# The spatial mixing of a gated block in three products of rounded halves instead of one f32 product

## The chip, the cores and the metric

The kernel runs on one core of a Trainium2 chip. The metric is the device time of one execution in microseconds; of three runs of the kernel before, the median was 1364.89 us (1363.35 to 1366.57).

## What is computed

Two transformer blocks on 512 tokens of width 1024. The change sits in the first layer of the first block, a gated MLP with spatial mixing:

```
u, v, z = split(h @ w_in, 3)                       # each 512 x 2048
u = gelu(u)
v = rms_norm(gelu(v), sgu_g)
v = v.reshape(1, 4, 128, 8, 256)                   # chunks of 128 tokens, 8 groups of 256 columns
mixed = einsum('gts,bcsge->bctge', tril(w_s), v) + b_s
y = u * mixed * silu(z)
return x + gate * (y @ w_out)
```

The mixing multiplies each group's columns of v, chunk by chunk of 128 tokens, with a lower triangular 128x128 matrix.

## The kernel before, in words

The program is written out per engine, with semaphores between the engines; no scheduler moves anything. TensorE, VectorE, ScalarE, GpSimd (called pool in the code) and the DMA queue of SyncE each have their own list of instructions, and each runs its list in order.

Large products are made of rounded halves. A tile a is split into a_hi, its value rounded to the float32r type, and a_lo = a - a_hi, and a product becomes three: hi with hi, hi with lo, lo with hi (`columns`, line 2187, and `split`, line 2178). ScalarE rounds a chunk of weights of 128x2048 (`to_hi`, line 678), VectorE subtracts (`to_lo`, line 1228).

The first layer goes in stages. The v stage makes 8 chunks of v in `v_pair` (line 2296); ScalarE applies gelu and sums the squares (`v_chunk`, line 750). Behind its last chunk ScalarE does four small operations on the statistics (lines 784 to 790), between which VectorE does its own (lines 1462 to 1469). Then comes the uz stage, 16 blocks j (the loop `uz_pair`, two blocks for each u, par = 0 and 1). In each block:

- TensorE (line 2338) waits for the chunk of weights and for free accumulators, makes u and z of 128 columns in two banks, 24 products of 512 columns each, then waits for v_staged and does the mixing into turn0 or turn1: for four chunks c of tokens one f32 product with v_stage as stationary and ws_t as moving operand.
- GpSimd (`stage`, line 621) makes the staged tile: v times its reciprocal rms, 128x512, into v_stage0 or v_stage1 by turns. It waits for the mixing of block j - 2 by the code.
- ScalarE (line 793) rounds the next chunk of weights, applies gelu to u into one of two gelu_u, tanh to z, and rounds the result y into y_hi.
- VectorE (line 1472) subtracts for the next chunk of weights (w_lo), does two units of the modulation (ada_units), multiplies the gates (tanh_z, then gelu_u), reads the mixing out of the bank with gain and bias (mixed), multiplies (line 1490), and subtracts y_hi (line 1492).

The triangular mask is put on ws_t by VectorE early in the v stage (line 1449), which raises ws_ready to 1. Ahead of the uz stage stands `pe.wait_ge(ws_ready, 1)` (line 2355). TensorE's `stay_busy` (line 2278) issues products on zeros at the start of the program.

```
for half in range(2):
    columns(G[2 * par + half][:, :], par, half, KT, h_hi, h_lo_of).then_inc(mm_done, 1)
pe.wait_ge(v_staged, j + 1)
ge(pe, mix_freed, j - 1)
for c in range(TB):
    mixed_c = mm((T0, T1)[par][:, P * c:P * c + P], v_stage[par][:, c, :], ws_t[:, u - W_UZ // 2, :], True, True)
mixed_c.then_inc(mix_done, 1)
```

Of the kernel before, what the change touches and what calls it, by code (L numbers as in the profile page):

```python
# [26 lines left out]
P = 128  # L27
TOK = 512
# [126 lines left out]
def program(nc, d):  # L155
# [4 lines left out]
    def at(name, shape, off, dt=F32):  # L160
        return nc.alloc_sbuf_tensor_at(name, shape, dt, offset=off)
# [85 lines left out]
    b_sp = at("b_sp", [P, GROUPS, P], off_blocks)  # L247
    gelu_u = [at(f"gelu_u{s}", [P, TOK], T[2 + s]) for s in range(2)]
    tanh_z = at("tanh_z", [P, TOK], T[4])
    mixed = [at(f"mixed{s}", [P, TOK], T[5 + s]) for s in range(2)]  # L250
    v_stage = [at(f"v_stage{s}", [P, TB, P], T[7 + s]) for s in range(2)]
    v_sq = at("v_sq", [P, TB, 256], T[2])
# [89 lines left out]
    def sem(name):  # L342
        return nc.alloc_semaphore(name)
# [11 lines left out]
    up_done, up_out, gsa_done = sem("up_done"), sem("up_out"), sem("gsa_done")  # L355
    xn_done, one_ready, idle_ready = sem("xn_done"), sem("one_ready"), sem("idle_ready")
    hi_done, lo_done, lo_half_done = sem("hi_done"), sem("lo_done"), sem("lo_half_done")
# [3 lines left out]
    sq_ready, sq_added, qsq_ready = sem("sq_ready"), sem("sq_added"), sem("qsq_ready")  # L361
    qlo_ready, half_zeroed, half_ready = sem("qlo_ready"), sem("half_zeroed"), sem("half_ready")
    sum_done, ln_done, y0_done, half_done = sem("sum_done"), sem("ln_done"), sem("y0_done"), sem("half_done")
# [6 lines left out]
    v_sums_done, v_stat_dve, v_stat_act = sem("v_sums_done"), sem("v_stat_dve"), sem("v_stat_act")  # L370
    v_staged, mix_done, mix_freed = sem("v_staged"), sem("mix_done"), sem("mix_freed")
    gelu_done, tanh_done, uz_done = sem("gelu_done"), sem("tanh_done"), sem("uz_done")
# [76 lines left out]
    def next_chunk(u, par):  # L449
        return (u, 1) if par == 0 else (u + 1, 0)  # L450
# [21 lines left out]
    with block:  # L472
# [146 lines left out]
        @block.gpsimd  # L619
        def _(pool):  # L620
            def stage(j, par):

                ge(pool, mix_done, j - 1)
                nc.gpsimd.tensor_tensor(v_stage[par][:, :, :], v[:, :, bass.ds(j * P, P)],
                                        v_stat[:, 5, :].unsqueeze(2).broadcast_to([P, TB, P]), ALU.mult).then_inc(v_staged, 1)

            def sum_squares(k, total, tile):

                for m in range(1, KT - 1):
                    pool.wait_ge(sq_ready, 8 * k + m + 1)  # L630
                    if m > 1:
                        pool.wait_ge(sq_added, 6 * k + m - 1)
                    nc.gpsimd.tensor_tensor(total, tile(0) if m == 1 else total, tile(m), ALU.add).then_inc(sq_added, 1)

            nc.gpsimd.memset(one_row[:, :], 1.0).then_inc(one_ready, 1)
            nc.gpsimd.memset(idle[:, :].bitcast(F32), 0.0).then_inc(idle_ready, 1)
            nc.gpsimd.memset(half_r[:, :].bitcast(F32), 0.0).then_inc(half_zeroed, 1)
            nc.gpsimd.memset(eps_tile[:, :], EPS)
            nc.gpsimd.memset(ones_r[:, :].bitcast(F32), 1.0).then_inc(ones_ready, 1)
            pool.wait_ge(half_zeroed, 1)  # L640
            pool.wait_ge(ones_ready, 1)
            for e in range(2):
                if e:
                    pool.wait_ge(half_ready, 1)
                part = slice(64 * e, 64 * e + 64)
                nc.gpsimd.memset(half_r[part, part].bitcast(F32), 1.0).then_inc(half_ready, 1)
            pool.wait_ge(half_ready, 2)
            pool.wait_ge(v_stat_dve, 3)
            stage(0, 0)
            stage(1, 1)  # L650
            with pool.Fori(1, AT // 2) as i:
                for par in range(2):
                    stage(2 * i + par, par)

            sum_squares(1, sq_sum[:, :], lambda m: sq_a[m % 2][:, :])

            def quarters(m):

                pool.wait_ge(exp_done, 4 * m + 4)
                ge(pool, spread_done, m)  # L660
                stats = row_stat[:, 0, :, :].rearrange("p k n -> p (k n)").unsqueeze(1).broadcast_to([P, 4, 16])
                nc.gpsimd.tensor_tensor(row_apart[:, :, :], stats, own_quarter.unsqueeze(2).broadcast_to([P, 4, 16]), ALU.mult).then_inc(apart_done, 1)

            pool.wait_ge(blocks_loaded, 16)
            for m in range(QH):
                quarters(m)
            pool.wait_ge(pv_done, 4 * QH)
            nc.gpsimd.memset(wf_hi[:, :, :].bitcast(F32), 0.0).then_inc(wf_zeroed, 1)
            nc.gpsimd.memset(wf_lo[:, :, :].bitcast(F32), 0.0).then_inc(wf_zeroed, 1)
            sum_squares(2, sq_sum[:, :], lambda m: sq[m % 2][:, :])  # L670
            sum_squares(3, sq_sum[:, :], lambda m: sq[m % 2][:, :])
# [3 lines left out]
        def _(act):  # L675
# [113 lines left out]
            act.wait_ge(lam_part, 2)  # L789
            nc.scalar.activation(lam_two[:, :], lam_two[:, :], ACT.Exp).then_inc(lam_exp, 1)  # L790


            def uz_pair(u):
                j = 2 * u - W_UZ
                for par in range(2):
                    to_hi(*next_chunk(u, par))
                    act.wait_ge(mm_done, 4 * u + 2 * par + 1)
                    ge(act, uz_done, j + par - 1)
                    nc.scalar.activation(gelu_u[par][:, :], G[2 * par][:, :], ACT.Gelu_apprx_tanh).then_inc(gelu_done, 1)
                    act.wait_ge(mm_done, 4 * u + 2 * par + 2)  # L800
                    ge(act, uz_done, j + par)
                    nc.scalar.activation(tanh_z[:, :], G[2 * par + 1][:, :], ACT.Tanh, scale=0.5).then_inc(tanh_done, 1)
                    act.wait_ge(y_done, j + par + 1)
                    nc.scalar.activation(y_hi[:, j + par, :], mixed[par][:, :], ACT.Copy).then_inc(yhi_done, 1)

# [415 lines left out]
        def _(dve):  # L1221
# [246 lines left out]
            dve.wait_ge(lam_exp, 1)  # L1468
            stt(neg_lam[:, :], lam_two[:, 1:2], -LAM_INIT, lam_two[:, 0:1], ALU.add, ALU.subtract).then_inc(lam_ready, 1)


            def uz_pair(u, cond):
                jj = 2 * u - W_UZ
                g = u - W_UZ // 2
                for par in range(2):
# [6 lines left out]
                    dve.wait_ge(acc_freed, 2 * j + 2)  # L1482
                    stt(gelu_u[par][:, :], tanh_z[:, :], 0.5, gelu_u[par][:, :], ALU.mult, ALU.mult).then_inc(uz_done, 1)
                    dve.wait_ge(mix_done, j + 1)
                    mix = mixed[par][:, :].rearrange("p (c t) -> p c t", c=TB)
                    stt(mix, (T0, T1)[par][:, :].rearrange("p (c t) -> p c t", c=TB), vecs[:, bass.ds(j + G_SGU, 1)],
                        b_sp[:, bass.ds(g, 1), :].broadcast_to([P, TB, P]), ALU.mult, ALU.add).then_inc(mix_freed, 1)
                    dve.wait_ge(mix_freed, j + 1)
                    dve.wait_ge(uz_done, j + 1)
                    nc.vector.tensor_tensor(mixed[par][:, :], mixed[par][:, :], gelu_u[par][:, :], ALU.mult).then_inc(y_done, 1)  # L1490
                    dve.wait_ge(yhi_done, j + 1)
# [682 lines left out]
        def _(pe):  # L2174
# [106 lines left out]

            pe.wait_ge(one_ready, 1)
            pe.wait_ge(c_loaded, 16)
            for n in range(2):
                mm(G[n][:, :], one_row[:, :], c_in[:, TOK * n:TOK * n + TOK], True, True).then_inc(c_spread_in, 1)
            pe.wait_ge(idle_ready, 1)
            stay_busy(6)
# [50 lines left out]
            def uz_pair(u):  # L2338
                jj = 2 * u - W_UZ
                for par in range(2):  # L2340
                    j = jj + par
                    chunk_ready(u, par)
                    if isinstance(u, int):
                        pe.wait_ge(v_gelu_done, 2 * (W_UZ - 2 + par) + 2)
                    else:
                        pe.wait_ge(acc_freed, 2 * j - 2)
                    for half in range(2):
                        columns(G[2 * par + half][:, :], par, half, KT, h_hi, h_lo_of).then_inc(mm_done, 1)
                    pe.wait_ge(v_staged, j + 1)
                    ge(pe, mix_freed, j - 1)  # L2350
                    for c in range(TB):
                        mixed_c = mm((T0, T1)[par][:, P * c:P * c + P], v_stage[par][:, c, :], ws_t[:, u - W_UZ // 2, :], True, True)
                    mixed_c.then_inc(mix_done, 1)

            pe.wait_ge(ws_ready, 1)
            uz_pair(W_UZ // 2)
# [255 lines left out]
            pe.wait_ge(wflo_done, 1)  # L2612
            pe.wait_ge(half_ready, 2)
            pe.wait_ge(acc_freed, 2 * W_Q2 - 16)
# [374 lines left out]
```

## Time and profile before

| what | value |
|---|---|
| median of the runs | 1364.89 us (1363.35 to 1366.57) |
| the profiled execution, by the same measure | 1366.15 us |
| its span, first to last instruction | 1364.4 us |
| matmuls and weight loads | 7883 each |
| DVE, ACT, POOL instructions | 1793, 1261, 55 |
| granted TensorE clock over the span | 1.000 |
| HBM traffic over the span | 132 GB/s |

PE is TensorE's matmul, PEld its weight loads, which overlap the matmuls; DVE is VectorE, ACT ScalarE, POOL GpSimd, SP the queue of SyncE. The duration of a matmul is modelled to its end in the pipeline and overlaps the next one's, so the distance between starts is what one costs in a row of them. An f32 product appears as two records, each with its weight load, a product of rounded values as one. Idle time of an engine that nobody waits for costs nothing. The times of timeline rows are counted from the start of the span.

### The profile page before, as it was taken

How to read it: one execution, taken by the hardware profiler on the slowest of the kernel's cores; microseconds unless marked ns; L12 is line 12 of the kernel's file. 1: busy time of each engine (PE TensorE's matmuls, PEld its weight loads, DVE VectorE, ACT ScalarE, POOL GpSimd, SP SyncE). 2: the span in 40 equal slices, each digit the busy share in tenths (PEclk: the TensorE clock that was granted, in tenths of full speed). 3: DMA queues.
4: the chain of work that ended last, by engine and by line, in shares of the span. 5: the costliest groups of instructions: out<-in, count | busy, mean ns of one | idle time of the engine just before them, and what ended most of it. 6: DMA issues, size and time to landing. Idle time of an engine off the chain costs nothing.

```text
span 1364.4 us, 21359 instructions
## 1 busy us (share of the span) xinstructions
PE 1356.1 (99%) x7883; PEld 1164.0 (85%) x7883; DVE 1060.6 (78%) x1793; ACT 718.5 (53%) x1261; POOL 50.9 (4%) x55
## 2 busy tenths in 40 slices
PE   8999999999999999999999999999999999999999
PEld 6998888888879878888888787887788998998997
DVE  6976677777799788888888867878878965983873
ACT  5744333223357666666664467667646642662561
POOL 0000000000100000000001100000030000000000
PEclk9999999999999999999999999999999999999999
DMA  9995455556753221111221231111131232333232
GB/s 378 388 354 187 178 184 184 184 185 262 292 193 105 79 81 62 63 63 61 65 88 64 93 124 62 62 63 63 37 118 62 94 132 78 103 122 124 77 111 92
DMA packets 35350, 181.51 MB, mean 133 GB/s; under 512 B 4153, under 2 KB 4921, under 8 KB 20930
## 3 DMA queue, kind: packets, MB, share of 16 engines
q1 hardware_dynamic: 34050, 177.95, 35.9%
q10 hardware_dynamic: 1216, 2.44, 0.5%
q8 instruction: 52, 0.85, 0.3%
q14 instruction: 32, 0.26, 0.1%
HBM read 177.74 MB, written 2.11 MB: 132 GB/s over the span
## 4 chain that ended last, share of the span: by engine, by line
PE 89%; DVE 4%; DMA 4%; issue 2%; ACT 1%; SPq 0%; DVEq 0%; ACTq 0%
PE acc L2176 66%; PE turn L2808 7%; PE ada L2176 4%; DMA ada_out<-in_ada 3%; PE turn L2176 3%; PE norm L2176 3%; PE ada L2808 2%; PE acc L2808 2%; PE norm L2808 2%; DVE w_lo L1234 1%; PE turn L2653 1%; PE turn L2499 1%; DVE hk_lo L1226 0%; DVE ada_out L1226 0%; DVE hx L1226 0%
## 5 line engine op out<-in xcount | busy, mean ns | idle before, releaser
L2176 PE MATMUL acc<-h_hi,w_hi 128*128 128x512 f32 x696 | 277.1, 398 | 0.0
L2176 PE MATMUL acc<-h_hi,w_lo 128*128 128x512 f32 x696 | 271.9, 391 | 0.0
L2176 PE MATMUL acc<-h_lo,w_hi 128*128 128x512 f32 x696 | 271.3, 390 | 0.0
L1234 DVE TENSOR_TENSOR w_lo<-w_raw,w_hi 128x2048 fp32r<-128x2048 f32 x58 | 136.4, 2352 | 29.9 <-ACT w_hi L683 29.9
L2176 PEld LDWEIGHTS acc<-h_hi,w_lo 128*128 128x128 f32 x696 | 130.6, 188 | 28.3
L2176 PEld LDWEIGHTS acc<-h_hi,w_hi 128*128 128x128 f32 x696 | 130.8, 188 | 27.0 <-issue 0.4
L2176 PEld LDWEIGHTS acc<-h_lo,w_hi 128*128 128x128 f32 x696 | 130.9, 188 | 25.5
L683 ACT ACTIVATE w_hi<-w_raw 128x2048 fp32r<-128x2048 f32 x60 | 114.4, 1907 | 29.0 <-PE acc L2176 28.2
L2176 PE MATMUL acc<-wv_hi,h_hi 128*128 128x256 f32 x320 | 90.5, 284 | 0.0
L1226 DVE SCALAR_TENSOR_TENSOR x<-acc,mods,x 128x512 f32<-128x512 f32 x48 | 38.7, 814 | 66.6 <-PE acc L2176 66.5
L2176 PE MATMUL acc<-wv_lo,h_hi 128*128 128x256 f32 x320 | 89.2, 280 | 0.0
L2176 PE MATMUL acc<-wv_hi,h_lo 128*128 128x256 f32 x320 | 88.4, 280 | 0.0
L689 ACT ACTIVATE y<-norm,eps_tile 128x512 f32<-128x512 f32 x54 | 37.2, 689 | 63.7 <-PE norm L2176 63.7
L2176 PE MATMUL acc<-gu_lo,w_hi 128*128 128x512 f32 x176 | 68.5, 389 | 0.0
L2176 PE MATMUL acc<-gu_hi,w_hi 128*128 128x512 f32 x176 | 68.5, 389 | 0.0
L2176 PE MATMUL acc<-gu_hi,w_lo 128*128 128x512 f32 x176 | 68.5, 389 | 0.0
L2176 PEld LDWEIGHTS acc<-wv_lo,h_hi 128*128 128x128 f32 x320 | 61.0, 190 | 0.2
L2176 PEld LDWEIGHTS acc<-wv_hi,h_hi 128*128 128x128 f32 x320 | 60.2, 188 | 0.2
L2176 PEld LDWEIGHTS acc<-wv_hi,h_lo 128*128 128x128 f32 x320 | 59.6, 188 | 0.0
L1226 DVE SCALAR_TENSOR_TENSOR ada_out<-ada_out,csil 128x1024 f32<-128x1024 f32 x32 | 38.4, 1221 | 18.3 <-DMA ada_out<-in_ada 18.0
L2176 PE MATMUL acc<-y_hi,w_hi 128*128 128x512 f32 x128 | 50.2, 392 | 0.0
L2176 PE MATMUL acc<-y_hi,w_lo 128*128 128x512 f32 x128 | 49.9, 390 | 0.0
(385 smaller groups left out, 3470.9 us busy)
## 6 DMA issues: line engine op xcount, KB each, us to landing
w_raw<-in_weights SPq DMA_DIRECT2D x102, 1024.0 KB, 4.9
ada_v<-in_ada SPq DMA_DIRECT2D x32, 512.0 KB, 6.1
ada_raw<-in_ada SPq DMA_DIRECT2D x32, 512.0 KB, 5.7
ada_out<-in_ada SPq DMA_DIRECT2D x32, 512.0 KB, 6.4
ada_up<-in_ada_first SPq DMA_DIRECT2D x8, 1024.0 KB, 16.9
w_raw<-in_weights SPq DMA_DIRECT2D x4, 768.0 KB, 4.4
x<-in_x SPq DMA_DIRECT2D x2, 1024.0 KB, 6.1
w_first<-in_weights SPq DMA_DIRECT2D x4, 512.0 KB, 13.6
```

The lines of the kernel that those rows point to most:

```text
L683: nc.scalar.activation(weights_at(u, par)[0][:, 0:used], w_raw[par][:, 0:used], ACT.Copy).then_inc(hi_done, 1)
L689: nc.scalar.activation(y0[:, :], total, ACT.Ln, scale=1.0 / count, bias=eps_col).then_inc(ln_done, 1)
L1226: return nc.vector.scalar_tensor_tensor(out, in0, scalar, in1, op0, op1, **more)
L1234: nc.vector.tensor_tensor(lo[:, 0:used], w_raw[par][:, 0:used], f32(hi[:, 0:used]), ALU.subtract).then_inc(lo_done, 1)
L2176: return nc.tensor.matmul(out, lhsT, rhs, start=start, stop=stop)
L2499: turned = nc.tensor.transpose((T0, T1)[c % 2][:, P * b:P * b + P], s_b[tile][:, lo:lo + P], ident)
L2653: turned = nc.tensor.transpose(T0[:, P * b:P * b + P], s_2[n % 3][:, 0, P * b:P * b + P], ident)
L2808: last = nc.tensor.matmul(out, w_part[:, n, :], a_part[:, n, :], start=start and n + m == 0, stop=stop and n + m == 5, skip_group_check=no ...
```

## The change

The mixing is made of rounded halves like the large products. ws_t gets a rounded half ws_hi (ScalarE) and a remainder ws_lo (VectorE), each raising ws_ready by one. The staged tile gets a rounded half v_stage_hi (ScalarE, semaphore v_rounded) and a remainder v_stage_lo (GpSimd, written over v_stage). TensorE does three products of 128 columns where it did one in f32. The staged tile lies where ws_t was, so the first staging waits for ws_ready = 3, and so does TensorE ahead of the uz stage. v_stage, gelu_u and mixed have one buffer each instead of two. Two semaphores are merged into others (fill_ready, half_ready), with no other effect on the order.

```diff
-    gelu_u = [at(f"gelu_u{s}", [P, TOK], T[2 + s]) for s in range(2)]
-    tanh_z = at("tanh_z", [P, TOK], T[4])
-    mixed = [at(f"mixed{s}", [P, TOK], T[5 + s]) for s in range(2)]
-    v_stage = [at(f"v_stage{s}", [P, TB, P], T[7 + s]) for s in range(2)]
+    gelu_u = at("gelu_u", [P, TOK], T[2])
+    tanh_z = at("tanh_z", [P, TOK], T[3])
+    mixed = at("mixed", [P, TOK], T[4])
+    v_stage = at("v_stage", [P, TB, P], big + 64 * KB)
+    v_stage_lo = at("v_stage_lo", [P, TB, P], big + 64 * KB, F32R)
+    v_stage_hi = at("v_stage_hi", [P, TB, P], big + 66 * KB, F32R)
+    ws_hi = at("ws_hi", [P, GROUPS, P], T[7], F32R)
+    ws_lo = at("ws_lo", [P, GROUPS, P], T[5], F32R)
...
             def stage(j, par):
-                ge(pool, mix_done, j - 1)
-                nc.gpsimd.tensor_tensor(v_stage[par][:, :, :], v[:, :, bass.ds(j * P, P)],
+                ge(pool, mix_done, j)
+                nc.gpsimd.tensor_tensor(v_stage[:, :, :], v[:, :, bass.ds(j * P, P)],
                                         v_stat[:, 5, :].unsqueeze(2).broadcast_to([P, TB, P]), ALU.mult).then_inc(v_staged, 1)
+                pool.wait_ge(v_rounded, j + 1)
+                nc.gpsimd.tensor_tensor(v_stage_lo[:, :, :], v_stage[:, :, :], v_stage_hi[:, :, :].bitcast(F32), ALU.subtract).then_inc(v_staged, 1)
...
             pool.wait_ge(v_stat_dve, 3)
+            pool.wait_ge(ws_ready, 3)
             stage(0, 0)
...
             nc.scalar.activation(lam_two[:, :], lam_two[:, :], ACT.Exp).then_inc(lam_exp, 1)
+            act.wait_ge(ws_ready, 1)
+            nc.scalar.activation(ws_hi[:, :, :], ws_t[:, :, :], ACT.Copy).then_inc(ws_ready, 1)
...
                 for par in range(2):
+                    act.wait_ge(v_staged, 2 * (j + par) + 1)
+                    nc.scalar.activation(v_stage_hi[:, :, :], v_stage[:, :, :], ACT.Copy).then_inc(v_rounded, 1)
                     to_hi(*next_chunk(u, par))
                     act.wait_ge(mm_done, 4 * u + 2 * par + 1)
-                    ge(act, uz_done, j + par - 1)
-                    nc.scalar.activation(gelu_u[par][:, :], G[2 * par][:, :], ACT.Gelu_apprx_tanh).then_inc(gelu_done, 1)
+                    nc.scalar.activation(gelu_u[:, :], G[2 * par][:, :], ACT.Gelu_apprx_tanh).then_inc(gelu_done, 1)
...
             stt(neg_lam[:, :], lam_two[:, 1:2], -LAM_INIT, lam_two[:, 0:1], ALU.add, ALU.subtract).then_inc(lam_ready, 1)
+            dve.wait_ge(ws_ready, 2)
+            nc.vector.tensor_tensor(ws_lo[:, :, :], ws_t[:, :, :], f32(ws_hi[:, :, :]), ALU.subtract).then_inc(ws_ready, 1)
...
-                    pe.wait_ge(v_staged, j + 1)
+                    pe.wait_ge(v_staged, 2 * j + 2)
                     ge(pe, mix_freed, j - 1)
+                    coarse, fine = ws_hi[:, u - W_UZ // 2, :], ws_lo[:, u - W_UZ // 2, :]
                     for c in range(TB):
-                        mixed_c = mm((T0, T1)[par][:, P * c:P * c + P], v_stage[par][:, c, :], ws_t[:, u - W_UZ // 2, :], True, True)
+                        out = (T0, T1)[par][:, P * c:P * c + P]
+                        mm(out, v_stage_hi[:, c, :], coarse, True, False)
+                        mm(out, v_stage_hi[:, c, :], fine, False, False)
+                        mixed_c = mm(out, v_stage_lo[:, c, :], coarse, False, True)
                     mixed_c.then_inc(mix_done, 1)
 
-            pe.wait_ge(ws_ready, 1)
+            pe.wait_ge(ws_ready, 3)
             uz_pair(W_UZ // 2)
```

In the built program the places are these. ScalarE between the v stage and the uz stage; a row is a line of code, the operation, what is written and what is read, and the semaphores it waits for. Before:

```order
L788 ACTIVATE v_stat<-v_stat 128x4 [waits v_stat_act]
L790 ACTIVATE lam_two<-lam_two 128x2 [waits lam_part]
L683 ACTIVATE w_hi_60<-w_raw_53 128x2048 [waits mm_done,w_loaded1]
L799 ACT_TABLE_LOAD
L799 ACTIVATE gelu_u_137<-acc 128x512 [waits mm_done]
L802 ACTIVATE tanh_z<-acc 128x512 [waits mm_done]
```

and with the change:

```order
L796 ACTIVATE v_stat<-v_stat 128x4 [waits v_stat_act]
L798 ACTIVATE lam_two<-lam_two 128x2 [waits lam_part]
L800 ACTIVATE ws_hi<-ws_t 128x1024 [waits ws_ready]
L807 ACTIVATE v_stage_hi<-v_stage 128x512 [waits v_staged]
L691 ACTIVATE w_hi_60<-w_raw_53 128x2048 [waits mm_done,w_loaded1]
L810 ACT_TABLE_LOAD
L810 ACTIVATE gelu_u<-acc 128x512 [waits mm_done]
```

Two roundings stand ahead of that of the next chunk of weights, w_hi.

TensorE at the start of the uz stage (acc are the banks of u and z, turn those of the mixing), with the change; before, the first row waits for the same three semaphores and in place of the twelve turn rows stand four of turn<-ws_t,v_stage:

```order
L2189 MATMUL acc<-h_hi,w_hi_59 128x512 [waits v_gelu_done,lo_done,ws_ready]
L2189 MATMUL acc<-h_lo,w_hi_59 128x512
L2189 MATMUL acc<-h_hi,w_lo_61 128x512
...
L2189 MATMUL turn<-ws_hi,v_stage_hi 128x128 [waits v_staged]
L2189 MATMUL turn<-ws_lo,v_stage_hi 128x128
L2189 MATMUL turn<-ws_hi,v_stage_lo 128x128
```

The wait for ws_ready stands on the first product of the stage in both programs; its value is now 3 where it was 1.

## Rows read from the trace of the kernel before

**Rows 1.** The page: busy us, share of the span and count of instructions, by engine.

```profile
PE 1356.1 (99%) x7883; PEld 1164.0 (85%) x7883; DVE 1060.6 (78%) x1793; ACT 718.5 (53%) x1261; POOL 50.9 (4%) x55
```

**Rows 2.** Stretches: length; busy us of PE, PEld, DVE, ACT, POOL; clock; DMA.

```profile
114.30:304.60 190.30, 190.30 (x904) 159.46 (x903) 133.19 (x162) 60.83 (x74) 16.62 (x16) 1.00 0.48 175
304.60:1364.40 1059.80, 1055.51 (x6245) 904.34 (x6243) 837.54 (x1480) 596.26 (x1066) 32.81 (x28) 1.00 0.28 101
```

**Rows 3.** Timeline of one block, TensorE: start, us, engine, line, operation, out<-in, count.

```profile
196.28 1.06 PE L2176 MATMUL turn<-ws_t,v_stage 128*128 x8
197.09 0.47 PE L2176 MATMUL acc<-h_hi,w_hi 128*128 128x512 f32 x1
...
197.40 0.39 PE L2176 MATMUL acc<-h_lo,w_hi 128*128 128x512 f32 x1
...
197.63 0.40 PE L2176 MATMUL acc<-h_hi,w_lo 128*128 128x512 f32 x1
...
208.92 0.47 PE L2176 MATMUL acc<-h_hi,w_hi 128*128 128x512 f32 x1
```

**Rows 4.** Timeline, TensorE around a product of 96 columns.

```profile
49.28 0.21 PE L2176 MATMUL acc<-ones_r 128*128 128x96 f32 x1
...
49.33 0.35 PE L2176 MATMUL acc<-wv_hi,h_hi 128*128 128x256 f32 x1
...
49.52 0.28 PE L2176 MATMUL acc<-wv_lo,h_hi 128*128 128x256 f32 x1
...
49.63 0.28 PE L2176 MATMUL acc<-wv_hi,h_lo 128*128 128x256 f32 x1
```

**Rows 5.** Timeline, TensorE's weight loads behind two products of 2 columns.

```profile
766.80 0.19 PEld L2176 LDWEIGHTS acc<-xg_hi,w_hi 128*128 128x128 f32 x1
766.91 0.19 PEld L2176 LDWEIGHTS acc<-xg_lo,w_hi 128*128 128x128 f32 x1
```

**Rows 6.** Timelines and one tile: start of the uz stage; operations of 128x1024.

```profile
114.41 0.40 PE L2176 MATMUL acc<-h_hi,w_hi 128*128 128x512 f32 x1
...
118.14 0.19 ACT L790 ACTIVATE lam_two<-lam_two 128x2 f32<-128x2 f32 x1
...
766.26 1.06 ACT L955 ACTIVATE w_hi<-w_raw 128x1024 fp32r<-128x1024 f32 x1 [0.76 <-PE acc L2176]
...
L1449 DVE TENSOR_TENSOR ws_t<-ws_t,consts x1: 1222/1222/1222, 59.6 to 59.6; 128x1024 f32<-128x1024 f32 x1
```

**Rows 7.** The start of the program: timeline of TensorE and its weight loads.

```profile
6.21 2.93 PE L2176 MATMUL ada<-idle 128*128 128x512 f32 x6
8.94 4.64 PE L2176 MATMUL norm<-sq_first,ones_r 128*128 128x512 f32 x8
...
9.81 0.34 PEld L2176 LDWEIGHTS norm<-sq_first,ones_r 128*128 128x128 f32 x1 [0.52 <-DVE sq_first L1421]
10.66 0.34 PEld L2176 LDWEIGHTS norm<-sq_first,ones_r 128*128 128x128 f32 x1 [0.52 <-issue]
11.27 0.19 PEld L2176 LDWEIGHTS norm<-sq_first,ones_r 128*128 128x128 f32 x1 [0.28 <-issue]
...
13.02 4.23 PE L2176 MATMUL ada<-idle 128*128 128x512 f32 x16
18.75 0.45 PE L2176 MATMUL acc<-w_first,h_full 128*128 128x256 f32 x1 [1.50 <-issue]
```

**Rows 8.** Timeline of the same block, the other engines; the last row is of block 15.

```profile
197.52 1.04 POOL L624 TENSOR_TENSOR v_stage<-v,v_stat 128x512 f32<-128x512 f32 x1 [10.79 <-PE turn L2176]
...
198.01 1.11 DVE L1226 SCALAR_TENSOR_TENSOR gelu_u<-tanh_z,gelu_u 128x512 f32<-128x512 f32 x1
...
200.63 0.63 ACT L804 ACTIVATE y_hi<-mixed 128x512 f32 x1 [3.48 <-DVE mixed L1490]
...
209.03 0.69 DVE L1226 SCALAR_TENSOR_TENSOR tanh_z<-tanh_z,acc 128x512 f32<-128x512 f32 x1 [1.26 <-ACT tanh_z L802]
...
304.37 0.69 DVE L1226 SCALAR_TENSOR_TENSOR gelu_u<-tanh_z,gelu_u 128x512 f32<-128x512 f32 x1
```

More of the change, by code:

```diff
@@ L355, in program @@
     up_done, up_out, gsa_done = sem("up_done"), sem("up_out"), sem("gsa_done")
-    xn_done, one_ready, idle_ready = sem("xn_done"), sem("one_ready"), sem("idle_ready")
+    xn_done, fill_ready = sem("xn_done"), sem("fill_ready")
     hi_done, lo_done, lo_half_done = sem("hi_done"), sem("lo_done"), sem("lo_half_done")
@@ L361, in program @@
     sq_ready, sq_added, qsq_ready = sem("sq_ready"), sem("sq_added"), sem("qsq_ready")
-    qlo_ready, half_zeroed, half_ready = sem("qlo_ready"), sem("half_zeroed"), sem("half_ready")
+    qlo_ready, half_ready = sem("qlo_ready"), sem("half_ready")
     sum_done, ln_done, y0_done, half_done = sem("sum_done"), sem("ln_done"), sem("y0_done"), sem("half_done")
@@ L370, in program @@
     v_sums_done, v_stat_dve, v_stat_act = sem("v_sums_done"), sem("v_stat_dve"), sem("v_stat_act")
-    v_staged, mix_done, mix_freed = sem("v_staged"), sem("mix_done"), sem("mix_freed")
+    v_staged, v_rounded = sem("v_staged"), sem("v_rounded")
+    mix_done, mix_freed = sem("mix_done"), sem("mix_freed")
     gelu_done, tanh_done, uz_done = sem("gelu_done"), sem("tanh_done"), sem("uz_done")
@@ L633, in sum_squares @@
                     nc.gpsimd.tensor_tensor(total, tile(0) if m == 1 else total, tile(m), ALU.add).then_inc(sq_added, 1)
-            nc.gpsimd.memset(one_row[:, :], 1.0).then_inc(one_ready, 1)
-            nc.gpsimd.memset(idle[:, :].bitcast(F32), 0.0).then_inc(idle_ready, 1)
-            nc.gpsimd.memset(half_r[:, :].bitcast(F32), 0.0).then_inc(half_zeroed, 1)
+            nc.gpsimd.memset(one_row[:, :], 1.0).then_inc(fill_ready, 1)
+            nc.gpsimd.memset(idle[:, :].bitcast(F32), 0.0).then_inc(fill_ready, 1)
+            nc.gpsimd.memset(half_r[:, :].bitcast(F32), 0.0).then_inc(half_ready, 1)
             nc.gpsimd.memset(eps_tile[:, :], EPS)
             nc.gpsimd.memset(ones_r[:, :].bitcast(F32), 1.0).then_inc(ones_ready, 1)
-            pool.wait_ge(half_zeroed, 1)
+            pool.wait_ge(half_ready, 1)
             pool.wait_ge(ones_ready, 1)
@@ L643, in _ @@
                 if e:
-                    pool.wait_ge(half_ready, 1)
+                    pool.wait_ge(half_ready, 2)
                 part = slice(64 * e, 64 * e + 64)
                 nc.gpsimd.memset(half_r[part, part].bitcast(F32), 1.0).then_inc(half_ready, 1)
-            pool.wait_ge(half_ready, 2)
+            pool.wait_ge(half_ready, 3)
             pool.wait_ge(v_stat_dve, 3)
+            pool.wait_ge(ws_ready, 3)
             stage(0, 0)
@@ L803, in uz_pair @@
                     act.wait_ge(y_done, j + par + 1)
-                    nc.scalar.activation(y_hi[:, j + par, :], mixed[par][:, :], ACT.Copy).then_inc(yhi_done, 1)
+                    nc.scalar.activation(y_hi[:, j + par, :], mixed[:, :], ACT.Copy).then_inc(yhi_done, 1)
             uz_pair(W_UZ // 2)
@@ L1482, in uz_pair @@
                     dve.wait_ge(acc_freed, 2 * j + 2)
-                    stt(gelu_u[par][:, :], tanh_z[:, :], 0.5, gelu_u[par][:, :], ALU.mult, ALU.mult).then_inc(uz_done, 1)
+                    stt(gelu_u[:, :], tanh_z[:, :], 0.5, gelu_u[:, :], ALU.mult, ALU.mult).then_inc(uz_done, 1)
                     dve.wait_ge(mix_done, j + 1)
-                    mix = mixed[par][:, :].rearrange("p (c t) -> p c t", c=TB)
+                    mix = mixed[:, :].rearrange("p (c t) -> p c t", c=TB)
                     stt(mix, (T0, T1)[par][:, :].rearrange("p (c t) -> p c t", c=TB), vecs[:, bass.ds(j + G_SGU, 1)],
@@ L1489, in uz_pair @@
                     dve.wait_ge(uz_done, j + 1)
-                    nc.vector.tensor_tensor(mixed[par][:, :], mixed[par][:, :], gelu_u[par][:, :], ALU.mult).then_inc(y_done, 1)
+                    nc.vector.tensor_tensor(mixed[:, :], mixed[:, :], gelu_u[:, :], ALU.mult).then_inc(y_done, 1)
                     dve.wait_ge(yhi_done, j + 1)
@@ L2280, in stay_busy @@
                     mm(AD[:, :], idle[:, 0:P], idle[:, :], True, True)
-            pe.wait_ge(one_ready, 1)
+            pe.wait_ge(fill_ready, 1)
             pe.wait_ge(c_loaded, 16)
@@ L2285, in _ @@
                 mm(G[n][:, :], one_row[:, :], c_in[:, TOK * n:TOK * n + TOK], True, True).then_inc(c_spread_in, 1)
-            pe.wait_ge(idle_ready, 1)
+            pe.wait_ge(fill_ready, 2)
             stay_busy(6)
@@ L2612, in _ @@
             pe.wait_ge(wflo_done, 1)
-            pe.wait_ge(half_ready, 2)
+            pe.wait_ge(half_ready, 3)
             pe.wait_ge(acc_freed, 2 * W_Q2 - 16)
```

## Prediction

> **What bounds the kernel now.** I read the page first: TensorE is busy 1356.1 us, 99% of the span, and VectorE as the next 78% [rows 1]. In the busy time by stretch, the gate-and-value stage that the change touches (114.3 to 304.6 us) has no idle TensorE time at all: 190.30 of 190.30 us busy, against VectorE's 133.19, ScalarE's 60.83 and GpSimd's 16.62 [rows 2]. After it TensorE idles only 1059.80 - 1055.51 = 4.3 us [rows 2]. So time added to TensorE's queue there goes into the end one for one, and at most 4.3 us of it could be recovered later. The timeline of one block shows what that queue holds: 48 products of 512 columns (the wide products), then mixing, in a period of 208.92 - 197.09 = 11.83 us [rows 3].
>
> **Part 1: the mixing products.** Removed per block: four f32 products, which the trace shows as eight passes. They occupy 196.28 to 197.09, 0.81 us, and the wide product behind them is followed after 0.31 us instead of 0.23 [rows 3]: together 0.89 us, 0.11 per pass. Added: twelve products of rounded halves, 128 columns each, each with its own weight load. No row of before has that shape, so I bound it.
> - From below, a 96-column product of rounded values was followed after 49.33 - 49.28 = 0.05 us. But the next product then took 0.19 us, where its like behind it took 0.11, so the two together have 0.12 each [rows 4]. As a mere column cost, twelve at 0.05 would be 0.60 us.
> - Behind two products of two columns, which hide nothing, the loads still stand at 766.80 and 766.91, 0.11 us apart [rows 5]. Twelve at 0.11 are 1.33 us.
> - From above, a product could cost what a wide one does, 0.23 us [rows 3]: 2.76 us.
>
> I take 0.11, because rows 4 and 5 both show a full rounded load setting the pace whenever the columns are few. That is +0.44 us per block, 16 blocks, **+7.1 us**. The bounds are 16 x (0.60 - 0.89) = -4.6 and 16 x (2.76 - 0.89) = +30 us. The 128-column weights now are always v_stage, and the first two products of a triple share them, but nothing suppresses the second load: the wide products repeat their weights in the same way and have one load record each.
>
> The Trainium skill speaks for the lower bound: "TensorE: Matmul & The Clock Gate", section on weight-path perf modes, has a fast weight load switched on for 128 weights of any type but FP32, by name not these. With its 55.6 ns for a warm 128-column product the mixing would be an estimated 0.67 us and the term -3.5 us. The 0.11 us between the loads in rows 5 speaks against it, and the measurement decides.
>
> **Part 2: the wait ahead of the stage.** TensorE's first wide product waits for ws_ready, now with the value 3: the order listing has it on that product, ahead of all 16 blocks and not on the first mixing. The value 1 was long there; 3 needs both halves of ws_t. TensorE started this stage at 114.41 [rows 6]. ScalarE gets to ws_hi only behind the four small statistics operations, the last of which runs from 118.14 to 118.33 [rows 6]. The rounding of 128x1024 costs 1.06 us, as the other one of this size [rows 6]: done at 119.4. VectorE then subtracts 128x1024, 1.22 us by the masking of the same tile [rows 6]: done near 120.7 with 0.1 for the two hand-overs. TensorE restarts near 120.8: **+6.4 us**. The bounds are 6.2 (no hand-over time at all) and 7.0 (0.25 us for each of the three hand-overs); it can hardly fail to appear, since nothing on ScalarE or VectorE moved ahead. Queued behind the wait are all the wide products of block 0, which need none of these tiles; so is, on GpSimd, the first staging, and on ScalarE behind that the rounding of the next weights. These land near 120.8 + 1.04, + 0.63, + 1.90 = 124.4 and VectorE's remainder (2.29) near 126.8, but TensorE wants them only at 120.8 + 10.9 + 1.3 = 133. Hidden.
>
> **Part 3: TensorE's pace after the gap.** 6.4 us without a product is longer than any gap after the start. What the trace has: the first dense run, behind the start's idle time, went at half pace: six products of 512 rounded columns in 8.94 - 6.21 = 2.73 us, 0.455 each, against 0.23 later [rows 3, 7]. The loads of the f32 passes behind them stand 0.85 us apart (9.81 to 10.66), then 0.61 (to 11.27), so the rise falls in there; sixteen products like the six took 4.23 us from 13.02 on, 0.26 each [rows 7]. By pace this is the 1.2 and then the 2.4 GHz level, although the granted clock reads 1.000 over the whole span, so here I go by the products. The next gap, 1.50 us ending at 18.75, was followed by a 256-column f32 pass of 0.45 us, which is the full pace, so it did no harm [rows 7]. So a restart costs between 0 and half of the time at half pace. At the start 6.2 to 11.0 was 4.8 us of dense work at half pace, half of it lost: **+2.4 us**. I take it, since the gap is four times the one that did no harm. The same page of the Trainium skill, in its part on the clock gate, also has the clock fall in an idle TensorE and return only under work; without that the term would be 0.
>
> **Part 4: the staging, beside the products.** GpSimd's product of 1.04 us starts 0.43 us into a block [rows 8], as before: it already waited for the previous mixing, so the single v_stage costs nothing. ScalarE rounds it (0.63, like y_hi [rows 8]) behind y_hi of the block before, 4.2 to 4.8 us into the block; GpSimd subtracts until about 5.9. TensorE needs it at 10.9: 5 us of cover. The rounding pushes the next weights' rounding (now 4.1 us in) and VectorE's chain behind it by 0.63. VectorE waited 1.26 us for tanh_z [rows 8], so 0.6 is left, plus 0.44 from the longer period. The single gelu_u and mixed are written only after operations that precede them in the same queues anyway. One hazard: VectorE's gelu_u product takes 1.11 us beside GpSimd's work and 0.69 where GpSimd is idle [rows 8]. The new subtraction falls between y_lo and w_lo, where VectorE idles; if it hit w_lo instead, 0.4 of the 0.6 would go. Priced at 0. If this cover were gone, every excess over 0.6 us would count 16 times.
>
> **Sum.** 7.1 + 6.4 + 2.4 = +15.9 us. The profiled execution took 1366.15 us (span 1364.4), so 1382.1 by its measure; the median of the runs is 1.3 lower, 1364.89, and gives **1380.8**.
>
> **The rivals.**
> 1. *The pace holds through the gap*: +13.5, 1378.4. For: the 1.50 us gap did no harm. Against: this one is four times as long. Chance 0.18.
> 2. *Narrow products priced by their columns, with loads that hide*: mixing 0.60 us, -4.6 + 6.4 + 2.4 = +4.2, 1369.1. This is the one that can end on the other side. With the pace held it is +1.8, 1366.7, which is no change. It decides from 0.055 us per product: then 16 x (0.66 - 0.89) = -3.7 brings the stall of 6.4 down to 2.7 us, which is 0.2%. For: the 0.05 of the 96 columns; against: the load spacing in rows 4 and 5. Chance 0.13, of which 0.05 with the pace held; another 0.01 is left for a gain that I do not see. This is the outcome that the Trainium skill's fast weight load, cited above, would lead to.
> 3. *Narrow products at a wide one's price*, if rounded values stream at full pace only in longer rows: +30 + 8.8, about 1404. The 96 columns in 0.05 us speak against. Chance 0.06.
> 4. *The staging becomes the bound*: ScalarE's extra rounding and GpSimd's subtraction eat VectorE's slack by 0.6 and 0.5, and the tanh_z product and what follows it come late enough that TensorE waits for a bank, perhaps 0.25 us per block: +4, 1385. Against: TensorE writes a bank again only two blocks on, some 12 us later. Chance 0.05.
>
> **The numbers.** About 0.2%, 2.7 us, is what a measurement of this kernel can tell from no change. The forecast has 0.57. Its own spread (stall 6.2 to 7.0; the pace term 1.2 to 3.6, a spread of half around 2.4 that I choose; 0.108 to 0.115 per product, so 6.5 to 7.8) is 1379 to 1383; with rival 1 and rival 4 the range is 1374.5 to 1387, which leaves out rivals 2 and 3. Slower: 0.57 + 0.18 + 0.08 (rival 2 with the gap's price) + 0.06 + 0.05 = **0.94**; within 0.2%: **0.05**; faster: **0.01**.
>
> **What would show it.** Right: TensorE's first wide product of the stage near 120.8, with the wait released by VectorE's ws_lo; the following products 0.45 us apart for some us, then 0.23; a mixing of about 1.25 us from its first product to the next wide one; a steady period of 12.27 us; VectorE waiting about 1 us for tanh_z, TensorE idle nowhere else in the stage. Wrong: mixing products 0.05 us apart (rival 2) or 0.2 and more (rival 3); products at 0.23 us right after the gap (rival 1); or idle time of TensorE before a mixing or a block, released by GpSimd, ScalarE or VectorE (rival 4).

## The result, and the profile after

The changed kernel takes 1381.83 us (median of 5 runs, 1378.07 to 1382.43) against 1364.89 us (5 runs, 1363.18 to 1367.51): ratio 1.0119, 95% interval [1.0106, 1.0133], which is 14.5 to 18.2 us more. The forecast was 1380.8. The profiled execution of the changed kernel took 1378.07 us, with a span of 1376.2 us, the fastest of the five; the other four left no trace. What differs between executions of one kernel ahead of this stage is told in the last section.

The page of the changed kernel, busy us and share by engine, answers to [rows 1]:

```profile
PE 1362.2 (99%) x7947; PEld 1170.7 (85%) x7947; DVE 1068.8 (78%) x1794; ACT 727.5 (53%) x1278; POOL 75.3 (5%) x71
```

TensorE is the bound as before, with 64 more records (12 for 8 in each of 16 blocks). GpSimd has 24 us more and ScalarE 9, and in the steady blocks TensorE waits for neither. Now the stretches (length; busy us of PE, PEld, DVE, ACT, POOL; granted clock; DMA share; GB/s): gap, restart, rest of block 0, steady blocks, and all behind the stage.

```profile
111.30:117.50 6.20, 0.22 (x2) 0.02 (x1) 1.81 (x5) 4.54 (x11) 0.00 (x0) 0.88 0.28 116
117.50:122.80 5.30, 5.28 (x12) 4.13 (x13) 1.62 (x1) 3.71 (x3) 2.33 (x2) 0.50 0.00 0
122.80:132.00 9.20, 9.20 (x47) 7.76 (x45) 3.02 (x6) 1.20 (x2) 0.00 (x0) 1.00 0.63 230
132.00:315.80 183.80, 183.80 (x906) 155.54 (x904) 134.78 (x152) 60.57 (x75) 36.85 (x30) 1.00 0.45 164
315.80:1376.20 1060.40, 1056.19 (x6250) 905.70 (x6249) 837.14 (x1481) 596.01 (x1066) 34.65 (x28) 1.00 0.29 101
```

A gap of 6.2 us without work, 5.3 us of work at a granted clock of 0.50, then full pace to the end. The 0.88 over the gap says that the clock fell inside it, some 1.5 us before its end (12% of 6.2 us, at half). Behind the stage nothing moved: 1060.4 us, where before the stretch from 303.53, the first product of the next stage, to the end was 1060.9 (the span of 1364.4 less 303.53). The gap's cause stands in the timeline of the start of the stage (start, us, engine, line, operation; in brackets the idle time and what ended it):

```profile
115.17 1.04 ACT L800 ACTIVATE ws_hi<-ws_t 128x1024 fp32r<-128x1024 f32 x1
...
116.25 1.22 DVE L1482 TENSOR_TENSOR ws_lo<-ws_t,ws_hi 128x1024 fp32r<-128x1024 f32 x1 [0.61 <-ACT ws_hi L800]
117.53 0.80 PE L2189 MATMUL acc<-h_hi,w_hi 128*128 128x512 f32 x1 [6.01 <-DVE ws_lo L1482]
...
118.12 0.63 PE L2189 MATMUL acc<-h_lo,w_hi 128*128 128x512 f32 x1
118.55 0.63 PE L2189 MATMUL acc<-h_hi,w_lo 128*128 128x512 f32 x1
...
122.39 0.60 PE L2189 MATMUL acc<-h_hi,w_lo 128*128 128x512 f32 x1
122.81 0.40 PE L2189 MATMUL acc<-h_hi,w_hi 128*128 128x512 f32 x1
123.05 0.39 PE L2189 MATMUL acc<-h_lo,w_hi 128*128 128x512 f32 x1
```

ScalarE's rounding, VectorE's subtraction, then TensorE: 0.43 us from product to product, until at 122.81 it becomes 0.23. The restart came at 117.53 and not near 120.8, because the whole stage began earlier in this execution than in that of before: its first product could have started at 111.35, where before it started at 114.41. One mixing in a steady block, which answers to [rows 3]:

```profile
204.41 0.22 PE L2189 MATMUL turn<-ws_hi,v_stage_hi 128*128 x1
204.47 0.28 PE L2189 MATMUL turn<-ws_lo,v_stage_hi 128*128 x1
204.58 0.27 PE L2189 MATMUL turn<-ws_hi,v_stage_lo 128*128 x1
204.69 0.28 PE L2189 MATMUL turn<-ws_hi,v_stage_hi 128*128 x1
...
205.58 0.28 PE L2189 MATMUL turn<-ws_hi,v_stage_lo 128*128 x1
205.70 0.45 PE L2189 MATMUL acc<-h_hi,w_hi 128*128 128x512 f32 x1
205.98 0.40 PE L2189 MATMUL acc<-h_lo,w_hi 128*128 128x512 f32 x1
...
217.93 0.45 PE L2189 MATMUL acc<-h_hi,w_hi 128*128 128x512 f32 x1
```

and the weight loads of its first three products:

```profile
204.19 0.19 PEld L2189 LDWEIGHTS turn<-ws_hi,v_stage_hi 128*128 128x128 f32 x1
204.41 0.19 PEld L2189 LDWEIGHTS turn<-ws_lo,v_stage_hi 128*128 128x128 f32 x1
204.52 0.19 PEld L2189 LDWEIGHTS turn<-ws_hi,v_stage_lo 128*128 128x128 f32 x1
```

The narrow products stand 0.11 us apart, from the second on each 0.06 behind the start of its own load. Only the first is followed after 0.06: its weights were loaded under a wide product (204.19), and the next load starts together with it (204.41). The wide product behind the mixing pays that back, being followed after 0.28 us instead of 0.23. The mixing runs 1.29 us to the next wide product where it was 0.81, and the period is 217.93 - 205.70 = 12.23 us where it was 11.83.

### The profile page after: what moved, and what is told of

Its sections match the earlier page's. It is cut to its first block, busy times and chain, and to the rows that moved or that the text cites. A ratio compares the mean times of both kernels' runs of the same rounds, so it can differ in the third digit from the quotient of the medians.

```text
span 1376.2 us, 21542 instructions
## 1 busy us (share of the span) xinstructions
PE 1362.2 (99%) x7947; PEld 1170.7 (85%) x7947; DVE 1068.8 (78%) x1794; ACT 727.5 (53%) x1278; POOL 75.3 (5%) x71
## 4 chain that ended last, share of the span: by engine, by line
PE 94%; DVE 4%; ACT 1%; issue 1%; DMA 0%; DVEq 0%; ACTq 0%
PE acc L2189 70%; PE turn L2825 7%; PE ada L2189 4%; PE turn L2189 4%; PE norm L2189 3%; PE ada L2825 2%; PE acc L2825 2%; PE norm L2825 2%; PE turn L2670 1%; PE turn L2516 1%; DVE hx L1237 0%; DVE fast_lo L2080 0%; DVE h_lo L1237 0%; DVE w_lo L2030 0%; DVE f_lo L2052 0%
## 5 line engine op out<-in xcount | busy, mean ns | idle before, releaser
L691 ACT ACTIVATE w_hi<-w_raw 128x2048 fp32r<-128x2048 f32 x60 | 114.4, 1907 | 29.0 <-PE acc L2189 28.2
L2189 PE MATMUL acc<-y_lo,w_hi 128*128 128x512 f32 x128 | 49.8, 389 | 0.0
```

The lines of the kernel that those rows point to most:

```text
L691: nc.scalar.activation(weights_at(u, par)[0][:, 0:used], w_raw[par][:, 0:used], ACT.Copy).then_inc(hi_done, 1)
L2189: return nc.tensor.matmul(out, lhsT, rhs, start=start, stop=stop)
```

## The experiments

Theory: three prices, and nothing else. A one-time gap (6.2 us), the half pace behind it (about 2.5), and per block four weight loads more, 0.41 us. The rivals: that the gap only hides a lateness which sits elsewhere too, that the pace falls for another reason, that columns and not loads set the price of the mixing, and that the staging or the single buffers take part. The kernel before, beside the first four, had a median of 1366.41 us (11 runs), and beside the last four of 1364.32 (27 runs). The same kernel thus reads 2.1 us apart in the two comparisons, so each ratio is to the kernel before beside it. The times in the last four expectations were set against 1366.4. A period below is the mean over eleven blocks from the fourth on.

**The halves of ws made early.** In `v_chunk`'s and `ada_v_units`' loops, instead of behind the statistics:

```diff
+                if u == 2:
+                    act.wait_ge(lam_part, 2)
+                    act.wait_ge(ws_ready, 1)
+                    nc.scalar.activation(ws_hi[:, :, :], ws_t[:, :, :], ACT.Copy).then_inc(ws_ready, 1)
...
+                    if (u, par) == (3, 0):
+                        dve.wait_ge(ws_ready, 2)
+                        nc.vector.tensor_tensor(ws_lo[:, :, :], ws_t[:, :, :], f32(ws_hi[:, :, :]), ALU.subtract).then_inc(ws_ready, 1)
```

> The changed kernel with ws_hi and ws_lo made in the v stage, some 30 us before they are needed; all else as in the change. Theory (the cost is a one-time gap, its half pace, and 12 loads for 8): the gap of 6.2 us and the 2.5 us lost at half pace go, only the mixing's 16 x 0.40 = 6.4 us stays: 1371.3 us, no idle TensorE time at the start of the uz stage, a period of 12.23 us. Rival (the gap is only moved, since the staging on GpSimd and the rounding on ScalarE come late anyway): TensorE waits before the first mixing or before block 1, 1375 to 1380.

Measured: 1371.74 us, ratio 1.0041 [1.0027, 1.0055] to before. TensorE waits for nobody from the v stage to the end of the uz stage; the period is 12.23. Gap and half pace are gone, 10.1 of the 16.9 us by the medians of two comparisons; the rest stays.

**TensorE's wait moved to the first mixing.**

```diff
-            pe.wait_ge(ws_ready, 3)
             uz_pair(W_UZ // 2)
...
+                    if isinstance(u, int) and par == 0:
+                        pe.wait_ge(ws_ready, 3)
                     pe.wait_ge(v_staged, 2 * j + 2)
```

> The changed kernel, with TensorE's wait for ws_ready = 3 moved from the head of the uz stage to the first mixing. Theory: as with the early halves, block 0's 48 products cover the making of the halves, so gap and half pace go: 1371.3 us. One thing could be late: VectorE's w_lo of block 1 was done 9.0 us behind ws_hi's start on the changed kernel, and TensorE now wants it about 8.5 us behind that, so a wait of up to 0.5 us before block 1: 1371.8. Rival (the gap sits before the first mixing or block 1 instead): 1374 and more.

Measured: 1370.10 us, ratio 1.0035 [1.0022, 1.0049]. Again no idle TensorE time in the stage, period 12.23. Making the halves is not what costs: block 0's wide products cover it. Only the place of the wait costs. The lateness before block 1, which I allowed up to 0.5 us for, did not come; it does come in the two runs below that shorten block 0's mixing.

**The f32 mixing with the wait.** The kernel before, plus the two roundings and the wait:

```diff
+    ws_hi = at("ws_hi", [P, GROUPS, P], big + 56 * KB, F32R)
+    ws_lo = at("ws_lo", [P, GROUPS, P], big + 60 * KB, F32R)
...
+            nc.scalar.activation(ws_hi[:, :, :], ws_t[:, :, :], ACT.Copy).then_inc(ws_ready, 1)
...
+            nc.vector.tensor_tensor(ws_lo[:, :, :], ws_t[:, :, :], f32(ws_hi[:, :, :]), ALU.subtract).then_inc(ws_ready, 1)
...
-            pe.wait_ge(ws_ready, 1)
+            pe.wait_ge(ws_ready, 3)
```

> The kernel before, with its f32 mixing and its double buffers, but ws_hi and ws_lo are made (and not used) at the place of the change, and TensorE waits for both ahead of the uz stage. Theory: it costs what the gap and the half pace behind it cost, 6.2 + 2.5 = 8.7 us, 1373.6 us, with a period of 11.83 us as before. Rival (the single buffers and the staging share in the cost of the start): less than 7 us. Rival (the pace is not the gap's doing): products 0.23 us apart at once, 1371.1.

Measured: 1372.65 us, ratio 1.0051 [1.0037, 1.0065]: 5 to 9 us, the theory's 8.7 being at its upper end. The median, 6.2 us over 1366.41, lies under the 7 us that the expectation gave to a share of the single buffers, so the times leave that rival open. The trace closes it, for it has the whole price without single buffers. Timeline, then the stretch of the restart, of this kernel:

```profile
117.94 0.79 PE L2182 MATMUL acc<-h_hi,w_hi 128*128 128x512 f32 x1 [6.37 <-DVE ws_lo L1475]
```

```profile
117.90:121.90 4.00, 3.96 (x9) 3.14 (x10) 3.80 (x2) 1.45 (x2) 0.88 (x1) 0.50 0.00 0
```

The same gap (6.4 us) and a clock of 0.50 behind it, here for 4.0 us and so 2.0 us lost (block 0 takes 131.71 - 117.94 = 13.8 us where it took 126.13 - 114.41 = 11.7), with the mixing, the period (11.83) and the buffers of the kernel before. The start's price belongs to the wait alone.

**The gap filled.** 24 wide products on data that is there, ahead of the wait:

```diff
+            for _ in range(24):
+                mm(AD[:, :], h_hi[:, 0, 0:P], h_hi[:, 0, :], True, True)
             pe.wait_ge(ws_ready, 3)
```

> The changed kernel, with 24 products of 512 columns on h_hi into the unused bank ada just ahead of the wait for ws_ready = 3 (24 x 0.227 = 5.4 us, less than the gap). Theory: TensorE starts block 0 at the same time as in the change, but at full pace, so 2.5 us are saved: 1379.3 us, granted clock 1.000. Rival (the half pace has another cause than the gap, as the data or the semaphore): the first products still 0.43 us apart, 1381.8.

Measured: 1377.04 us, ratio 1.0088 [1.0073, 1.0104], 4.8 us under the changed kernel's median (forecast 2.5; the two medians come from different comparisons and the runs of each spread over 3 to 4 us). The trace is what decides. Timeline of this kernel:

```profile
112.03 5.62 PE L2189 MATMUL ada<-h_hi 128*128 128x512 f32 x24
118.21 0.50 PE L2189 MATMUL acc<-h_hi,w_hi 128*128 128x512 f32 x1 [0.56 <-DVE ws_lo L1482]
118.55 0.39 PE L2189 MATMUL acc<-h_lo,w_hi 128*128 128x512 f32 x1
118.78 0.40 PE L2189 MATMUL acc<-h_hi,w_lo 128*128 128x512 f32 x1
```

Same wait, same releaser, same time lost to it, but the products go 0.23 us apart at once. Block 0 with its mixing takes 130.51 - 118.21 = 12.3 us against 14.8 in the changed kernel: 2.5 us, as the theory has it. The mean granted clock is 1.000 in all five executions, where the changed kernel has 0.996 to 0.998.

**The gap filled by half.** As the last, with 12 products.

> As the filled gap, with 12 products instead of 24: TensorE idles some 3.3 us instead of 6. Two readings of the gap's second price: it comes with any idle time of microseconds, then block 0 starts at half pace again and the time is 1379 to 1382; or it needs the longer gap, then the products are 0.23 us apart at once and the time is that of the filled gap, 1377. I expect the second in most executions.

Measured: 1376.63 us (4 runs), ratio 1.0088 [1.0072, 1.0103], the time of the filled gap. Timeline of the profiled execution, then the stretch of the restart, of this kernel:

```profile
117.86 0.50 PE L2189 MATMUL acc<-h_hi,w_hi 128*128 128x512 f32 x1 [3.28 <-DVE ws_lo L1482]
118.20 0.40 PE L2189 MATMUL acc<-h_lo,w_hi 128*128 128x512 f32 x1
```

```profile
117.80:123.00 5.20, 5.14 (x22) 4.24 (x23) 1.48 (x2) 3.73 (x3) 2.34 (x2) 1.00 0.01 3
```

Here 3.3 us of idleness left the clock at 1.00, where 6.0 and 6.4 us brought it to 0.50. But this holds for two of the four executions only. The profiled one and another have a mean granted clock of 1.000 and took 1376.00 and 1375.95 us; the other two have 0.998 and 0.999 and took 1377.48 and 1377.26 us, some 1.4 us more. By their clocks these two paid at least part of the second price, though without a trace the place is not shown. So the expected "in most executions" is not borne out: half filled, this gap went either way, and only the full filling kept the clock in every execution.

**Two products of three.** The kernel with the wait at the mixing, without v_stage_hi times ws_lo, which is left out of the computation:

```diff
                         mm(out, v_stage_hi[:, c, :], coarse, True, False)
-                        mm(out, v_stage_hi[:, c, :], fine, False, False)
                         mixed_c = mm(out, v_stage_lo[:, c, :], coarse, False, True)
```

> The kernel with TensorE's wait at the first mixing, without the middle one of the three products (v_stage_hi with ws_lo is left out of the computation): eight rounded products of 128 columns per block instead of twelve. Theory (a weight load of 0.111 us per product sets the pace): 16 x 4 x 0.111 = 7.1 us less, 1363.3 us; a mixing that costs 8 x 0.111 = 0.89 us as the eight f32 passes did, so no slower than the kernel before. Rival (columns set it, 0.05 us each): 3.2 us less, 1367.

Measured: 1364.71 us (11 runs), ratio 0.9999 [0.9990, 1.0008]: as fast as the kernel before, and no more. Over the 1366.41 that it was set against, the expectation comes to 0.998 for loads and to 1.000 for columns, so the median alone sides with the columns. The period decides against them: it is 11.79, so four products are 12.23 - 11.79 = 0.45 us (0.446 before rounding), 0.112 each and not 0.05. From its first product to the end of its last mixing the stage takes 303.70 - 114.65 = 189.06 us, against 307.72 - 111.98 = 195.74 with the wait moved: 6.7 us less, of the 7.1 expected. The rest is a wait before block 1, where TensorE now idles 0.3 us for w_lo. What the median lacks against this is not shown. Eight rounded products of 128 columns cost what the eight f32 passes did, within 0.04 us per block.

**Three wide products.** The kernel with the wait at the mixing; the halves of ws as stationary operand, v_stage as moving one; what comes out is turned and uses only the first group's matrix, so it is not the mixing:

```diff
-                    for c in range(TB):
-                        out = (T0, T1)[par][:, P * c:P * c + P]
-                        mm(out, v_stage_hi[:, c, :], coarse, True, False)
-                        mm(out, v_stage_hi[:, c, :], fine, False, False)
-                        mixed_c = mm(out, v_stage_lo[:, c, :], coarse, False, True)
+                    out = (T0, T1)[par][:, :]
+                    rows_hi, rows_lo = [tile[:, :, :].rearrange("p c n -> p (c n)") for tile in (v_stage_hi, v_stage_lo)]
+                    mm(out, ws_hi[:, 0, :], rows_hi, True, False)
+                    mm(out, ws_lo[:, 0, :], rows_hi, False, False)
+                    mixed_c = mm(out, ws_hi[:, 0, :], rows_lo, False, True)
```

> The kernel with TensorE's wait at the first mixing, its twelve products of 128 columns made three of 512 with the halves of ws as stationary operand (always the first group's, and the result is turned: what is computed is not the mixing). The columns are the same, 1536 per block; the weight loads are 3 instead of 12. Theory (loads set the pace of the narrow products): 3 x 0.227 = 0.68 us instead of 1.29, 16 x 0.61 = 9.8 us less, 1360.3 us, faster than the kernel before. Rival (columns set it): no change, 1370.1.

Measured: 1363.07 us (11 runs), ratio 0.9990 [0.9981, 1.0000]: faster than the kernel before by 0.1%, where the expectation comes to 0.4% (1360.3 to 1366.41). Its rival, no change from the run with the wait moved, would be 1.0035. In the profiled execution (1361.66 us) the mixing is the expected size (timeline):

```profile
146.70 0.40 PE L2189 MATMUL turn<-v_stage_hi,ws_hi 128*128 128x512 f32 x1
146.94 0.40 PE L2189 MATMUL turn<-v_stage_hi,ws_lo 128*128 128x512 f32 x1
147.18 0.40 PE L2189 MATMUL turn<-v_stage_lo,ws_hi 128*128 128x512 f32 x1
147.41 0.39 PE L2189 MATMUL acc<-h_hi,w_hi 128*128 128x512 f32 x1
```

0.71 us for the same 1536 columns that take 1.29 us in twelve pieces; the period is 11.61 against 12.23, and 16 of these differences are 10 us. The columns are the same and the loads are a quarter: not columns but loads set the price of the narrow products. Each product here has its own load, so the counts of these two runs can't tell a price per load from a price per product; what speaks for the load is the first narrow product of each mixing, which had its weights in time and is followed after 0.06 us. The whole stage takes 298.30 - 111.87 = 186.43 us, 9.3 less than with the wait moved, a wait of 0.4 us for w_lo before block 1 included; behind the stage this execution is 0.9 us longer (1061.6 against 1060.7). Why the median saves less than the profiled execution is not shown.

**The staging alone.** Single buffers, ScalarE's rounding and GpSimd's subtraction in each block with TensorE waiting for both, but f32 mixing and no halves of ws (v_stage, v_stage_hi and v_stage_lo apart, at T[5] to T[7]):

```diff
-            pe.wait_ge(ws_ready, 3)
+            pe.wait_ge(ws_ready, 1)
...
+                        mixed_c = mm((T0, T1)[par][:, P * c:P * c + P], v_stage[:, c, :], ws_t[:, u - W_UZ // 2, :], True, True)
```

> The staging of the change alone: single v_stage, gelu_u and mixed, ScalarE's rounding and GpSimd's subtraction in every block, TensorE waiting for both, but the mixing in f32 from v_stage and no halves of ws (the staged halves are made and not used). Theory: all of it is covered, the time is that of the kernel before, 1366.4 us, within 1.5; the period stays 11.83. Rival (the staging chain takes part in the slowdown): 0.1 us per block or more, 1368 and above, with idle time of TensorE ahead of a mixing or a block.

Measured: 1364.75 us (11 runs), ratio 1.0003 [0.9994, 1.0012], period 11.83, TensorE never idle in the stage. All of the staging and all three single buffers together cost nothing that the times can tell, about 0.1%, and nothing in the period.

No kernel here beats the one before and computes the mixing. With 128 columns and the tile as stationary operand, three rounded products need twelve loads where the f32 form has eight passes at the same price each; the order that needs three loads delivers tokens where the gates have columns.

## Why the prediction was right

- *What bounds the kernel*: as read. TensorE stayed 99% busy, all the added time is in its queue, and none of it was recovered behind the stage.
- *Part 1*, +7.1 us: right in kind, 0.6 too much. The steady period grew by 12.23 - 11.83 = 0.41 us (0.406 before rounding), 6.5 us in 16 blocks. The step that took 0.11 us from [rows 4, 5] instead of the 96-column product's 0.05 is confirmed at 0.112 by the two-product run, and the wide one shows that the columns are not the price. With the 0.05 us that the wide product behind it loses, the new mixing costs 1.34 us, where 1.33 was forecast. Mis-sized is what the f32 mixing took away with it: the forecast counted 0.08 us on one wide product behind it, but the 48 wide products of a block, which are the same in both kernels, take 11.02 us before and 10.95 with the change, several of them in the trace of before being followed after 0.23 to 0.24 us instead of 0.227. The Trainium skill's rule on fast weight loads ("TensorE: Matmul & The Clock Gate", weight-path perf modes), read as covering these operands, would have made this term an estimated gain of 3.5 us; the measured 0.11 us per load is against it, and that section's gain is not to be counted on for float32r.
- *Part 2*, +6.4 us: measured 6.2, from where TensorE's next product would have started (111.24 + 0.11) to 117.53, released by VectorE's ws_lo. The f32 kernel with the same wait has the same kind of gap (6.4 us), and moving the wait removes it.
- *Part 3*, +2.4 us: the products 0.43 us apart lasted from 117.53 to 122.81; block 0 took 132.30 - 117.53 = 14.8 us against 12.2 with the wait moved (111.98 to 124.17), 2.6 us. I inferred the fall from products alone; this trace shows it as a granted clock of 0.50. That the size fits is partly luck: 2.4 was half of one stretch at the start of the program, and the two traces with the long gap have 5.3 and 4.0 us of products at half pace behind it. The mean granted clock of the changed kernel's five executions also varies, 0.996 to 0.998; as an estimate, 0.001 of 1380 us is 2.8 us at half clock, so this price differs between executions. The clock gate part of the Trainium skill's page "TensorE: Matmul & The Clock Gate" agrees with these traces, in that idleness brings the clock down and only work brings it back.
- *Part 4*, 0: right, though two sizes in it were off. GpSimd's subtraction takes 1.43 us (I used 1.04), and VectorE's gelu_u product beside GpSimd's multiplication 1.57 us (1.11 before). The cover held: VectorE still waits 0.75 us for tanh_z.

```profile
205.34 0.69 DVE L1237 SCALAR_TENSOR_TENSOR tanh_z<-tanh_z,acc 128x512 f32<-128x512 f32 x1 [0.75 <-ACT tanh_z L813]
206.06 1.57 DVE L1237 SCALAR_TENSOR_TENSOR gelu_u<-tanh_z,gelu_u 128x512 f32<-128x512 f32 x1
...
210.38 1.43 POOL L632 TENSOR_TENSOR v_stage_lo<-v_stage,v_stage_hi 128x512 fp32r<-128x512 f32 x1 [3.30 <-ACT v_stage_hi L807]
```

- *Sum*: 6.5 + 6.2 + 2.6 = 15.3 us from the trace, 15.9 forecast, 14.5 to 18.2 measured. The spans of the two profiled executions differ by 11.8 us only: the stage could begin 3.1 us earlier in that of the changed kernel, and the stretch behind the stage was 0.5 us shorter.
- *The rivals*: the pace did not hold through the 6 us gap, though it did through 3.3 us in the profiled execution and, by the mean clocks, in two of four; narrow products cost neither their columns nor a wide one's price; the staging never became the bound.

## What to carry to other kernels

Where the moving operand is narrow, count weight loads and not columns: here a full load cost 0.11 to 0.12 us under 2, 96 or 128 columns, and splitting an f32 product of 128 columns into three rounded ones raised the count from 8 to 12. Put a wait directly ahead of the instruction that needs it: more than half of this slowdown (8.8 of 15.3 us in the trace) was one semaphore value ahead of 48 products that did not need it, and it took the clock with it. If a gap of that length can't be avoided, products on idle data can keep the pace, if there are enough of them: 24 (5.6 us) kept the clock in five executions of five, 12 (2.9 us) in two of four. They do not give the gap itself back.

## What the runs showed of the hardware

The 256-column products of rounded values in the v stage run at one of two spacings. Timelines of two kernels whose programs do not differ before their first mixing, first the one with two products, then the one with the wait moved:

```profile
113.59 0.28 PE L2189 MATMUL acc<-wv_hi,h_hi 128*128 128x256 f32 x1
113.70 0.28 PE L2189 MATMUL acc<-wv_lo,h_hi 128*128 128x256 f32 x1
113.82 0.28 PE L2189 MATMUL acc<-wv_hi,h_lo 128*128 128x256 f32 x1
113.94 0.28 PE L2189 MATMUL acc<-wv_hi,h_hi 128*128 128x256 f32 x1
```

```profile
111.53 0.28 PE L2189 MATMUL acc<-wv_hi,h_lo 128*128 128x256 f32 x1
111.64 0.28 PE L2189 MATMUL acc<-wv_hi,h_hi 128*128 128x256 f32 x1
111.76 0.28 PE L2189 MATMUL acc<-wv_lo,h_hi 128*128 128x256 f32 x1
111.87 0.28 PE L2189 MATMUL acc<-wv_hi,h_lo 128*128 128x256 f32 x1
```

Averaged over 100 to 109 us, three of the ten profiled executions (the kernel before, the early halves, the two products) have 0.118 us between products and the other seven 0.113. The uz stage could start at 114.4 to 114.7 us in the three and at 111.4 to 112.1 in the seven. Over the 576 products of the v stage the spacing makes 0.0045 x 576 = 2.6 us of this; the rest is in the work ahead of them. So of the 5.1 us between the two differences of before and after, 11.8 us by the spans of the profiled executions and 16.9 by the medians, 3.1 can come from there, since the trace of before has 0.118 and that of after 0.113. Which spacing the other executions had is not shown. The cause is open; nothing was tried on it. The wide products of a steady block do not show it: 0.228 us on average in both of these traces.

The granted clock reads 1.00 at the start of the program, where [rows 7] has products at half pace, but 0.50 behind the gap. So ahead of the first change that the profile records, that column can't be relied on, and the distance between like products can.
